# Layer-norm sums of the second token half on TensorE alone, weight splits by halves, and one attention sum moved by a block

## What is computed

```
# block 1, mixer 0: causal attention with stick-breaking weights, 16 heads of 64 (8 pairs of heads)
y = mixer_stick_breaking(h, sb_win)
h = layer_norm(2**0.25 * h + y @ mix_wo, ...)
h = layer_norm(2**0.25 * h + mem_cross_attn(h, mem, ...), ...)
h = layer_norm(2**0.25 * h + conv_ffn(h, ...), ...)     # width 2816; ends with "@ w_down"
# block 2
x = h
hn = x * rsqrt(mean(x * x) + 1e-6) * pre_norm_w          # rms_norm
p = hn @ w_in                                            # then an RWKV branch, a convolution, a pool, gates
```

## Time and profile before

| | us |
|---|---|
| median of 3 runs | 1488.82 (1488.02 to 1488.83) |
| the profiled execution's own time | 1487.92 |
| its span in the profile | 1486.2 |
| TensorE busy | 1428.9 (96%) |
| VectorE, ScalarE, GpSimd busy | 630.3, 626.5, 767.5 |

### The profile page before, as it was taken

The page is one execution under the profiler, slowest core; times in us unless marked ns, Lnnn a source line. Parts: engine busy times, 40 slices in busy tenths (PEclk is TensorE's granted clock), DMA queues, the critical chain, the costliest instruction groups (busy, mean ns, idle before and its releaser), DMA issues.

```text
span 1486.2 us, 22929 instructions
## 1 busy us (share of the span) xinstructions
PE 1428.9 (96%) x8960; PEld 1170.0 (79%) x8960; DVE 630.3 (42%) x780; ACT 626.5 (42%) x1054; POOL 767.5 (52%) x603
## 2 busy tenths in 40 slices
PE   7999999999998999999999799899999999999997
PEld 5887777677776888888888787688878888888886
DVE  5455544543255333333535856332337343111123
ACT  5555455534335444444322466343335333222342
POOL 4444444355345666666656446753326655544563
PEclk9999999999999999999999899999999999999999
DMA  5222222221122222222333212100012322222222
GB/s 200 86 85 75 81 71 86 70 99 58 57 73 70 99 100 99 92 91 99 104 108 100 85 57 85 57 17 3 3 39 96 119 89 95 91 98 99 99 99 71
DMA packets 35508, 122.92 MB, mean 83 GB/s; under 512 B 3936, under 2 KB 6240, under 8 KB 35296
## 3 DMA queue, kind: packets, MB, share of 16 engines
q1 hardware_dynamic: 34848, 119.64, 23.8%
q10 hardware_dynamic: 576, 2.06, 0.4%
HBM read 119.59 MB, written 2.10 MB: 82 GB/s over the span
## 4 chain that ended last, share of the span: by engine, by line
PE 79%; DVE 13%; ACT 5%; POOL 2%; issue 1%; DMA 0%; POOLq 0%; SPq 0%; ACTq 0%; DVEq 0%
PE ps L502 16%; PE ps L504 16%; PE ps L503 16%; PE ps L1153 2%; PE ps L1155 2%; PE ps L1154 2%; PE ps L1124 2%; DVE later_lo L2045 2%; DVE keep_lo L2032 2%; DVE keep L2027 2%; PE ps L1229 1%; PE ps L1231 1%; PE ps L1230 1%; DVE later_hi L2043 1%; PE ps L1110 1%; PE ps L591 1%
## 5 line engine op out<-in xcount | busy, mean ns | idle before, releaser
L1800 POOL TENSOR_TENSOR w_lo<-stage,w_hi 128x512 fp32r<-128x512 f32 x430 | 604.7, 1430 | 539.3 <-ACT w_hi L1260 539.2
L502 PE MATMUL ps<-x_hi,w_lo 128*128 128x512 f32 x904 | 357.5, 395 | 5.0 <-POOL w_lo L1800 5.0
L504 PE MATMUL ps<-x_hi,w_hi 128*128 128x512 f32 x904 | 352.9, 390 | 0.0
L503 PE MATMUL ps<-x_lo,w_hi 128*128 128x512 f32 x904 | 352.6, 390 | 0.0
L1260 ACT ACTIVATE w_hi<-stage 128x512 fp32r<-128x512 f32 x430 | 245.8, 621 | 63.9 <-DMA stage<-w 56.4
L502 PEld LDWEIGHTS ps<-x_hi,w_lo 128*128 128x128 f32 x904 | 170.2, 188 | 42.4 <-DVE rw_vz L2296 5.9
L503 PEld LDWEIGHTS ps<-x_lo,w_hi 128*128 128x128 f32 x904 | 170.2, 188 | 35.9 <-issue 1.7
L504 PEld LDWEIGHTS ps<-x_hi,w_hi 128*128 128x128 f32 x904 | 170.0, 188 | 36.1
L2155 DVE SCALAR_TENSOR_TENSOR conv<-ps,vcol,conv 128x511 f32<-128x511 f32 x44 | 33.0, 749 | 141.4 <-ACT conv L1426 141.4
L1426 ACT ACTIVATE conv<-ps,vcol 128x512 f32<-128x512 f32 x44 | 34.2, 779 | 131.1 <-PE ps L504 128.7
L2475 DVE TENSOR_TENSOR bt<-gates,ps 128x512 f32<-128x512 f32 x24 | 16.3, 679 | 143.7 <-PE ps L1231 143.7
(11 more groups left out here) (417 smaller groups left out, 2739.3 us busy)
## 6 DMA issues: line engine op xcount, KB each, us to landing
stage<-w SPq DMA_DIRECT2D x215, 512.0 KB, 3.2
outT<-H SPq DMA_DIRECT2D x16, 128.0 KB, 1.8
H<-xT SPq DMA_DIRECT2D x3, 512.0 KB, 8.1
mem<-memT SPq DMA_DIRECT2D x2, 512.0 KB, 10.4
extra_stage<-w SPq DMA_DIRECT2D x2, 512.0 KB, 5.1
pool_n<-pool_count ACTq DMA_DIRECT2D x1, 1024.0 KB, 5.8
H<-xT SPq DMA_DIRECT2D x2, 256.0 KB, 4.9
w_small<-small ACTq DMA_DIRECT2D x1, 512.0 KB, 4.4
```

The source lines that it names most:

```text
L502: pe.matmul(out, wl, hi(k), start=first, stop=False)
L503: pe.matmul(out, wh, lo(k), start=False, stop=False)
L504: mm = pe.matmul(out, wh, hi(k), start=False, stop=end)
L1800: pool.tensor_tensor(unit_lo(b)[:, cols], unit_stage(b)[:, cols], unit_hi(b)[:, cols].bitcast(F32), ALU.subtract).then_inc(wlo_made, 1)
```

## The change

1. In attention pairs 0 to 6, `later_sums(g, 1)` stands ahead of channel block 4 and no longer of block 3.
2. DVE no longer adds the second half of the last tile to the five running sums. TensorE sums the seven tiles' running sums for that half (`joint_early`, five matmuls), and adds the last tile straight from `Y` and `sqv` (`joint_y_sums`, three matmuls; `joint_square_sums`, two), the weighted ones with a matrix `mean_g` that already holds the channel's factor. DVE makes the three `mean_g` matrices (128 x 128) once, before the down projection's first tile.
3. The sums of the first half, `joint_sums(0)`, stand six matmuls earlier in `down_half(1)`.
4. DVE's chain of the first half is reordered: block 0 is scaled before `joint_mean`, block 1 after it, and `joint_y` of the second half comes ahead of block 2. In `FIRST`, (0, 2) comes before (1, 0).
5. ACT and POOL split units 1 and 2 by halves between the blocks (ACT behind blocks 0, 1, 3, 4; POOL behind 1, 2, 4, 5), and units 3 and 4 at the end: ACT behind blocks 6 and 7, POOL behind all eight blocks.

```diff
+        mean_g = at("mean_g", [P, 3, P], 27.75)
...
                 product(ps[:, 0, :], u + 3, (u + 3) % RING, x_rows, x_rows_lo,
-                        between={3: lambda: later_sums(g, 1), 6: turns})
+                        between={4: lambda: later_sums(g, 1), 6: turns})
...
+            def joint_early():
+
+                for at_n, src in ((MU, acc), (VAR, acc2), (GB, acc5), (GY, acc4), (ROOT2, acc3)):
+                    pe.matmul(joint_place(1, at_n), C("mean"), src[:, HALF[1]], start=at_n in (MU, GB, GY), stop=False,
+                              skip_group_check=True)
+
+            def joint_late(src, table):
+
+                for at_n, m in table:
+                    pe.matmul(joint_place(1, at_n), m, src, start=False, stop=True, skip_group_check=True).then_inc(sums_done, 1)
+
+            def joint_y_sums():
+                pe.wait_ge(y_made, BEFORE["y_made"]["down"] + CREDIT + KB + 1)
+                joint_late(Y[:, KB - 1, HALF[1]], ((MU, C("mean")), (GB, mean_g[:, 2, :]), (GY, mean_g[:, 1, :])))
+
+            def joint_square_sums():
+                pe.wait_ge(sq_made, BEFORE["sq_made"]["down"] + KB + 1)
+                joint_late(sqv[:, (KB - 1) % 2, HALF[1]], ((VAR, C("mean")), (ROOT2, mean_g[:, 0, :])))
...
-                        if half and (c, k) == (1, 1):
-                            joint_sums(0)
+                        if half and (c, k) == (0, 7):
+                            joint_sums()
...
-            FIRST = [(0, 0), (0, 1), (1, 0), (1, 1)] + [(n, k) for k in range(2, KB) for n in range(2)] + [(n, k) for n in range(2, 5) for k in range(KB)]
+            FIRST = [(0, 0), (0, 1), (0, 2), (1, 0), (1, 1), (1, 2)] + [(n, k) for k in range(3, KB) for n in range(2)] +                 [(n, k) for n in range(2, 5) for k in range(KB)]
...
-            rw_halves(0, FIRST, {FIRST.index((1, 0)): lambda: pe.wait_ge(y_made, BEFORE["y_made"]["down"] + CREDIT + KB + 1),
-                                 FIRST.index((0, 6)): lambda: joint_sums(1),
+            joint_early()
+            rw_halves(0, FIRST, {FIRST.index((0, 1)): joint_y_sums,
+                                 FIRST.index((1, 0)): joint_square_sums,
...
             joint_root(0, 0, ROOT)
+            h_made_of(0, 0)
             joint_root(0, 1, ROOT2)
-            h_made_of(0, 0)
             h_made_of(0, 1)
             for k in range(KB):
                 x_hi_of(0, k)
                 if k + 2 < KB:
                     h_made_of(0, k + 2)
-                if k == 1:
+                if k == 0:
                     joint_square(1)
                     act.dma_start(w_small[:], small.rearrange("p (a n) -> p a n", n=SEQ)).then_inc(small_in_s, 16)
-                if k == 6:
+                if k in (0, 1):
+                    split_hi(U0["rwkv"] + 1, parts=[k])
+                if k in (3, 4):
+                    split_hi(U0["rwkv"] + 2, parts=[k - 3])
+                if k == 5:
                     joint_mean_square(1)
-                if k in (0, 2, 5, 7):
-                    split_hi(U0["rwkv"] + 1 + (0, 2, 5, 7).index(k))
+                if k >= 6:
+                    split_hi(U0["rwkv"] + k - 3)
...
             for k in range(KB):
                 x_lo_of(0, k)
-                if k in (0, 2, 5, 7):
-                    split_lo(U0["rwkv"] + 1 + (0, 2, 5, 7).index(k))
+                if k in (1, 2):
+                    split_lo(U0["rwkv"] + 1, parts=[k - 1])
+                if k in (4, 5):
+                    split_lo(U0["rwkv"] + 2, parts=[k - 4])
+            for t in range(3, 5):
+                split_lo(U0["rwkv"] + t)
...
-            dve.tensor_scalar(gcol[:, 4, :], gcol[:, 1, :], -1.0, None, ALU.mult).then_inc(acc_made, 1)
+            link(dve.tensor_scalar(gcol[:, 4, :], gcol[:, 1, :], -1.0, None, ALU.mult))
+            for n, c in enumerate((0, 3, 4)):
+                ins = dve.tensor_scalar(mean_g[:, n, :], C("mean"), gcol[:, c, KB - 1:KB], None, ALU.mult)
+            ins.then_inc(acc_made, 1)
...
             joint_moments(0)
-            joint_centre(0, 1)
+            dve.wait_ge(rstd_made, 1 + BEFORE["rstd_made"]["down"])
+            joint_scale(0, 0)
             joint_mean(0)
-            joint_scale(0, 0)
-            joint_scale(0, 1)
+            joint_block(0, 1)
+            dve.wait_ge(unit_done, U0["rwkv"] + CREDIT)
+            joint_y(KB - 1, HALF[1], DOWN_BANK[1], KB)
             joint_block(0, 2)
             joint_x(0, 0)
             for k in range(3, KB):
                 joint_block(0, k)
                 joint_x(0, k - 2)
-                if k == 3:
-                    dve.wait_ge(unit_done, U0["rwkv"] + CREDIT)
-                    joint_y(KB - 1, HALF[1], DOWN_BANK[1], KB)
-                if k == 5:
-                    joint_add(KB - 1, HALF[1], KB)
```

26 lines of the change are left out of this document (13 added, 13 removed).

## The result

The changed kernel takes **1479.14 us** (median of 4 runs, 1478.3 to 1480.47), the kernel before beside it 1488.51 (4 runs, 1488.02 to 1488.83): ratio 0.9936, 95% interval 0.9923 to 0.9948, 9.4 us less. The forecast was 1477.9 with a range of 1476.0 to 1481.6. The profiled execution of the changed kernel is the slowest of its four (1480.47, span 1478.6); the one of before was its fastest (1487.92, span 1486.2), so the two profiles lie only 7.6 us apart.

The account below looks back on a forecast made before the run. TensorE, busy 96% of the span, was taken as the bound, so gains lie only where it waits or runs at the low clock. Attention 3.5 plus seam 7.4 made 10.9 us, giving 1477.9 us, range 1476.0 to 1481.6.

Parts of the forecast that it names:

- Attention: Attention pairs: sums put behind block 3 shorten TensorE's wait by 0.5 us a pair, 3.5 us over seven pairs.
- First half's sums six matmuls earlier: Seam, down projection: sums start 0.7 us earlier, mostly lost again waiting to form the second half's `Y`; gain 0.1 us.
- The adds leave DVE: Seam, last tile: without 5.44 us of adds, blocks follow at 1.24 us and the eighth `joint_x` ends near 837.4.
- Ten sums on TensorE: Seam: ten sum matmuls run while TensorE waits anyway, so they cost nothing.
- POOL becomes the bound: Seam, first half: POOL never idle from 832.45 to 847.4; `SECOND` starts at 851.25 instead of 858.70, 7.4 us gained.
- The second half: After the seam's first half: DVE instructions may take 1 us longer beside POOL; 6 us of lead cover it.
- The clock: TensorE at the seam: no pause over 1.7 us, so the high clock level is taken as kept.
- the first rival: Seam: TensorE drops to 1.2 GHz in pauses before 836.4; gain 9.5 us, time 1479.3, chance 0.24.
- The attention's wait only moves: Attention: the wait in `turns` takes back all, the seam alone gives 7.4 us; 1481.4, chance 0.07.
- POOL is slower: Seam: POOL's halves take 1.46 us, its 14.3 us become 17.1; gain 8.1, time 1480.7, chance 0.07.
- Slower than before: Seam: TensorE stays at 1.2 GHz from 836.5 through both halves; 9.7 us slower, 1498.5, chance 0.03.
- It doesn't do what it says: Seam: unit 4's `w_lo` is late by more than the adds cost; within the 0.04 for gains under 3 us.

Follow-up runs that it names:

- attn_only: Kernel before with only the attention's edit, the head-1 sums of `later_lo` one block later: 1485.62 us, ratio 0.9979, 3.0 us less.
- old_chain: Changed kernel with the old order of DVE's and ACT's chain put back, the new order of splits kept: 1478.95 us, ratio 0.9924.
- early_unit1: Changed kernel with weight unit 1 split before block 0 on ACT and POOL: 1479.54 us, ratio 0.9935.
- pool_more: Changed kernel with 2.5 us more work on POOL, two subtractions between the splits of units 3 and 4: 1483.58 us, ratio 0.9960.
- sums_only: Changed kernel with everything undone but the second half's sums (adds off DVE, ten sum matmuls on TensorE): 1484.70 us, ratio 0.9975.
- old_splits: Changed kernel with ACT's and POOL's weight splits put back as whole units after blocks 0, 2, 5 and 7: 1481.50 us, ratio 0.9953.
- the second set of runs: The changed kernel itself, unaltered, run again beside three other versions: 1478.72 us, ratio 0.9933.

## Why the prediction was right, and where it wasn't

**Attention, forecast 3.5 us, bounds 0 and 4.8.** Right in mechanism and size: attn_only gives 3.0 us; the transposes come 2.15 us after the first sum, where 2.2 to 2.3 were expected, and the wait for ACT's exponential took the wait's place. The wait for `later_lo` was left at 0.4 in this pair, where I had 0.3. The term was 0.5 us too large against the median, which is less than the interval can tell; the pairs themselves gained 3.1 in the profile.

**First half's sums six matmuls earlier, 0.1 us.** Right as far as it went: the first `joint_x` comes 1.38 us after the down projection, and came 1.36 after it before. I saw that the 0.7 us are lost again to the wait for `Y`, and left it at that. old_chain shows that not moving `Y` keeps them: 0.74.

**The adds leave DVE.** The pace of 1.24 us and the early eighth `joint_x` (836.31, its end 836.8; forecast near 837.4) are right. **The step that failed** is what the 7.4 us were credited to; the total did not hang on it, since the reckoning went through POOL's new order piece by piece. I gave them to the adds, with the splits' new order as a neutral part ("On the way unit 1 is ready at 836.35 ... the delay costs nothing"). The runs show 3.9 us for the sums alone and 2.4 for the new order of the splits (2.8 on the stretch), of which the text knew nothing. The reason was in the trace: on POOL an `x_lo` behind a whole unit waits 2.5 us, so with DVE faster, `x_lo` becomes what TensorE waits for, and the low clock followed those waits of 2.1 to 2.3 us. I had asked when each unit is ready, and not when each `x_lo` is. Nor did I ask why the five adds took 5.44 us: the same five on the first half, with POOL idle, took 1.96 (last section). So 3.5 us of what left DVE was there only beside POOL's work.

**Ten sums on TensorE, nothing.** Right: all ten lie in pauses. That they also keep the clock up, as the paragraph on the clock said, fits the rows, but no run has the adds gone without them.

**POOL becomes the bound.** Right: POOL has no pause from the second `x_lo` on, waits stand at units 1 and 3 (1.38 and 0.39 us; forecast 0.6 at unit 3), and it ends at 846.18 (forecast 847.4, with a start 1.1 us later than the real one, 831.30 for 832.45). Moving two of its pieces into its idle time shortens the stretch (early_unit1), adding work lengthens it by more than the work (pool_more). The seam's 7.4 us were 6.9 in the first profile, 7.3 in the second, and 6.9 in the medians: from the first joint sum to `lora` 45.3 and 44.95 us, forecast 44.8.

**The second half.** "One or two DVE instructions with both inputs in SBUF now run beside POOL and may take 1 us longer; the 6 us of lead cover it." The kind was right, the size five times too small, and the cover just held: the lead shrank from 6 us to 0.75 (`x_hi` out at 849.39, its first matmul at 850.14). I had priced the neighbour by the time of one POOL instruction, and it waited behind four. The second instruction, the `tensor_scalar`, I hadn't counted as one of the kind at all.

**The clock.** The forecast said it is kept, the rival that it falls in part. In the changed kernel it stays at 1.00 through the seam, in both profiles. In the seam a wait of 1.38 us left it up, while waits of 2.13 (sums_only), 2.32 (old_splits) and 1.93 (pool_more) were each followed by 0.50 to 0.64. That is no fixed rule of the wait's length: near 331 every profile has the same wait of 2.23 us, and the clock fell behind it in eight and stayed up in six (last section). The Trainium skill (TensorE: Matmul & The Clock Gate, section on HAM oscillation) says that pauses between bursts of matmuls bring the clock down; in those three kernels the trace agrees, and in the changed one the short pauses of the seam left it up. The page's own case has longer waits than that seam, so its rule did not in fact bring the first rival's 9.5 us.

**The rivals.** "The attention's wait only moves" is refuted by attn_only. "POOL is slower": its halves take 1.27 to 1.32 us, not 1.46. "Slower than before" and "It doesn't do what it says" did not happen. The first median, 1479.14, lies at the first rival's number, 1479.3, without its mechanism, since the clock stayed up in the seam. The 1.5 us between the two medians and the forecast's gain are of the size that the clock gives or takes elsewhere (last section): the second set of runs, at 10.8 us, hits the forecast's 10.9, and that closeness is in part luck.

## What to carry to other kernels

- When the engine that set the pace gets faster, look at the queue of the next one for small urgent pieces behind long ones. Here the new order of POOL's pieces took 2.8 us off the stretch at the same total work, beside 4.5 for taking 5.4 us of adds off DVE. Whether it was the halves or the two whole units moved to the end was not separated.
- Price a wait on TensorE twice: its length, and what the clock may take after it. 1.93 us of waiting came to 3.3 in pool_more; the second part is a chance and no sum, since one and the same wait of 2.23 us was followed by the low clock in eight profiles and not in six.
- Before moving work off an engine, ask why it takes so long there: the five adds took 5.44 us beside POOL's work and 1.96 with POOL idle. No run here tried to keep them on DVE away from POOL's splits; that rival of the change stands untested.
- Undo each part of a change that was made as a bundle. One part of this one (the reordered chain) gave nothing, and its profile says that it costs 0.9 us.
